# A chunked recurrence whose chain, output statistics and transposes are spread over the next pair's solver levels, with VectorE and ScalarE doing GpSimd's eight operations

## The reference

```python
def step(state, inp):                       # one token, 16 heads of 64
    r_t, w_t, k_t, v_t, kk_t, a_t = inp
    sa = jnp.einsum('bhij,bhj->bhi', state, -kk_t)
    state = (state * w_t[:, :, None, :]
             + sa[..., None] * (kk_t * a_t)[:, :, None, :]
             + v_t[..., :, None] * k_t[..., None, :])
    return state, jnp.einsum('bhij,bhj->bhi', state, r_t)
_, y = lax.scan(step, state0, (r, decay, k, v, kk, a))
y = ((y - mean) * lax.rsqrt(var + RW_GN_EPS)) * gn_w + gn_b   # per head
y = (y + sum(r * k * r_k) * v) * g
```

## Time and profile before

| what | us |
|---|---|
| median of 3 runs | 2706.45 (2702.31 to 2707.59) |
| the profiled execution's own time | 2708.74 |
| its span, first to last instruction | 2706.9 |
| TensorE busy | 2434.5 (90% of the span) |
| VectorE busy | 1606.1 (59%) |
| ScalarE busy | 634.9 (23%) |
| GpSimd busy | 563.5 (21%) |
| granted TensorE clock, mean of the span | 0.948 of full speed |

### The profile page before, as it was taken

How to read it: one execution, slowest core, us unless ns; L and a number is a source line. 1 busy time by engine, 2 the same in 40 slices (tenths; PEclk the granted TensorE clock), 3 DMA queues, 4 the chain that set the end, 5 groups by cost and what they waited for, 6 DMA issues and landing times. The chain is left out here.

```text
span 2706.9 us, 44357 instructions
## 1 busy us (share of the span) xinstructions
PE 2434.5 (90%) x16952; PEld 1977.2 (73%) x16952; DVE 1606.1 (59%) x2182; ACT 634.9 (23%) x1246; POOL 563.5 (21%) x382
## 2 busy tenths in 40 slices
PE   7999977987888869999999699999849898999998
PEld 6888865765666657888877588888638687788887
DVE  6646569945666545656556465656536565565654
ACT  3100012223545322101012310101435453210001
POOL 3212135421212102302030021213111300221213
PEclk9999997998999979999999799999969899999999
DMA  4333222430000012333325333332351101333331
GB/s 133 103 94 101 82 74 71 128 110 29 16 30 16 17 33 78 96 99 101 94 78 163 106 101 94 93 99 73 113 130 37 37 2 32 94 103 91 103 87 66
DMA packets 375943, 216.95 MB, mean 80 GB/s; under 512 B 18880, under 2 KB 359808, under 8 KB 375776
## 3 DMA queue, kind: packets, MB, share of 16 engines
q1 hardware_dynamic: 367648, 198.83, 26.0%
q10 hardware_dynamic: 8128, 15.83, 1.6%
HBM read 198.73 MB, written 15.89 MB: 79 GB/s over the span
## 5 line engine op out<-in xcount | busy, mean ns | idle before, releaser
L143 DVE TENSOR_TENSOR w_lo_ffn<-w_raw,w_hi_ffn 128x1024 fp32r<-128x1024 f32 x272 | 508.7, 1870 | 9.4
L387 POOL TENSOR_TENSOR act_ffn<-gated_ffn,usc_ffn 128x512 f32<-128x512 f32 x88 | 128.1, 1456 | 1007.4 <-ACT gated_ffn L367 1007.4
L367 ACT ACTIVATE gated_ffn<-gsc_ffn 128x512 f32<-128x512 f32 x88 | 55.8, 634 | 1010.4 <-DVE gsc_ffn L292 1010.4
L150 PE MATMUL p_gate_ffn<-hhi_ffn,w_hi_ffn 128*128 128x512 f32 x704 | 278.2, 395 | 7.6 <-DVE hlo_ffn L205 7.6
L150 PE MATMUL p_up_ffn<-hhi_ffn,w_hi_ffn 128*128 128x512 f32 x704 | 274.6, 390 | 2.9 <-DVE w_lo_ffn L143 2.9
L151 PE MATMUL p_gate_ffn<-hlo_ffn,w_hi_ffn 128*128 128x512 f32 x704 | 277.2, 394 | 0.0
L150 PE MATMUL p_down_ffn<-ahi_ffn,w_hi_ffn 128*128 128x512 f32 x704 | 274.9, 390 | 2.4 <-DVE x_res L303 2.4
L152 PE MATMUL p_gate_ffn<-hhi_ffn,w_lo_ffn 128*128 128x512 f32 x704 | 276.9, 393 | 0.0
L292 DVE TENSOR_TENSOR gsc_ffn<-p_gate_ffn,rstd_ffn 128x512 f32<-128x512 f32 x88 | 60.9, 692 | 363.6 <-PE p_up_ffn L152 363.0
L151 PE MATMUL p_up_ffn<-hlo_ffn,w_hi_ffn 128*128 128x512 f32 x704 | 274.6, 390 | 0.0
L152 PE MATMUL p_up_ffn<-hhi_ffn,w_lo_ffn 128*128 128x512 f32 x704 | 274.5, 390 | 0.0
(11 more groups left out here) (341 smaller groups left out, 4490.5 us busy)
## 6 DMA issues: line engine op xcount, KB each, us to landing
w_raw<-in_ffn_w_gate_dram SPq DMA_DIRECT2D x88, 512.0 KB, 3.8
w_raw<-in_ffn_w_up_dram SPq DMA_DIRECT2D x88, 512.0 KB, 3.8
w_raw<-in_ffn_w_down_dram SPq DMA_DIRECT2D x64, 512.0 KB, 4.1
w_raw<-in_ffn_w_down_dram SPq DMA_DIRECT2D x32, 384.0 KB, 3.4
w_raw<-in_rw_w_rkv_dram SPq DMA_DIRECT2D x24, 512.0 KB, 4.5
rkv_scratch<-staged_mix ACTq DMA_DIRECT2D x24, 256.0 KB, 2.5
w_raw<-in_kv_w_dram SPq DMA_DIRECT2D x12, 512.0 KB, 4.7
w_raw<-in_rw_w_o_dram SPq DMA_DIRECT2D x8, 512.0 KB, 5.4
```

The source lines that it names most:

```text
L143: nc.vector.tensor_tensor(lo, raw, fp(hi), ALU.subtract).then_inc(s["w_ready"], 1)
L150: nc.tensor.matmul(out, whi, hi, start=first, stop=False)
L367: nc.scalar.activation(gated[:], gsc[:, j], ACT.Silu).then_inc(s["silu"], 1)
L387: nc.gpsimd.tensor_tensor(act32[:], gated[:], usc[:, j], ALU.mult).then_inc(s["act32"], 1)
```

## The change

The recurrence is written anew as one schedule for each engine.
- The six links of pair p-1's chain, the state's part of its output and its centering now stand between the level operations of pair p. The variance of pair p-2's output comes after pair p's scores; its logarithm, exponential, normalization and gate come later in the same step; the rounded parts of pair p-3 come in level 0.
- The transposes of pair p (`turn`) are in its own levels 0 to 2, no longer in the chain of the pair before. One of them is written as 16 matmuls with an identity, so that its output lies crossed.
- Head 1's operands are put on the crossed partition halves (`side`), so that a group of 16 matmuls touches all four quadrants. One operation then serves both heads: one product, one copy, and one addition each for x and xt in a level, in separate banks.
- The first factor is an identity written ahead by ScalarE (`preset`) and four `copy_predicated` of VectorE, one of them from eight (64-column) matmuls more. Masks are applied for one level at a time (`part`). The identity in `ft` is added by 16 matmuls, and ScalarE copies `ft`.
- The mean is taken off by one matmul with a centering matrix; ScalarE squares and copies from its bank. VectorE adds the state's part to the part from inside the chunks.
- GpSimd has no block here. Of its six products VectorE takes three (`keys`, `rate_keys`), ScalarE three (as activations with scale and bias); VectorE takes the low part of the output too. ScalarE also takes the affine step after tanh from VectorE (`sg`).
- r, k, v and the weight slices have semaphores of their own and are loaded one by one. VectorE, ScalarE and TensorE wait for all constants at the start of the stage.
- The `Fori` loops in `mix_project`, `project_add` and `attention` become Python loops, so their bodies are written out.

The core of the diff:

```diff
+        def side(h, b):
+            return half(b if h == 0 else 1 - b)
...
+            def product(p, level):                       # TensorE
+                at(pe, p, "part", level + 1)
+                if level == 0:
+                    at(pe, p, "xin", 4)
+                else:
+                    at(pe, p, "x", level)
+                for t in range(NT):
+                    for b, h in quarters:
+                        m = mm(bank[side(h, b), A0 + h, cols(t)], parts[half(b), level, h, t], x[h][half(b), t], start=True, stop=True)
+                m.then_inc(s["g_mm"], 1)
...
+            def step(p):                                 # TensorE
+                scores(p); variance(p - 2); product(p, 0); chain(p - 1, 1); turn(p, 0); update(p, 0)
+                lak_v(p); chain(p - 1, 2); product(p, 1); rates(p + 1); chain(p - 1, 3); update(p, 1)
+                turn(p, 1); chain(p - 1, 4); product(p, 2); key_norm(p + 1); gate(p + 1); chain(p - 1, 5); update(p, 2)
+                turn(p, 2); chain(p - 1, 6); product(p, 3); carried(p - 1, (1, 2, 3, 4)); carried(p - 1, (5, 6, 7)); update(p, 3)
+                values(p + 1); product(p, 4); bonus(p + 1); centered(p - 1); update(p, 4); solve(p); outer(p)
...
+            def step(p):                                 # ScalarE
+                key_square(p + 1); product(p, 0); turned(p, 0); lak_v(p); rounded(p - 3); product(p, 1)
+                rates(p + 1); turned(p, 1); product(p, 2); gate(p + 1); logs(p + 1); logs_of_output(p - 2)
+                turned(p, 2); product(p, 3); roots(p + 1); decays(p + 1); roots_of_output(p - 2); values(p + 1)
+                product(p, 4); squares(p - 1); solved(p); preset(p + 1); outer(p)
...
+            def step(p):                                 # VectorE
+                scores(p); part(p, 0); key_scores(p); part(p, 1); rounded(p - 3); update(p, 0)
+                state(p - 1, 1); part(p, 2); state(p - 1, 2); update(p, 1); state(p - 1, 3); part(p, 3); state(p - 1, 4)
+                sums(p + 1); keys(p + 1); update(p, 2); state(p - 1, 5); key_norm(p + 1); state(p - 1, 6); centers(p + 1)
+                update(p, 3); part(p, 4); carried(p - 1); bonus_terms(p + 1); normalized(p - 2); gated(p - 2)
+                rate_keys(p + 1); rows_of_query(p + 1); update(p, 4); bonus(p + 1); rows_of_key(p + 1); outer(p)
...
-            with pe.Fori(0, 2) as i:                     # attention, and likewise on the other engines
+            for i in range(2):
```

More of the change, by code:

```diff
@@ new lines, in outer, with chain @@
+                m.then_inc(s["z_mm"], 1)
+            def chain(p, c):
+                if not 0 <= p < ND:
+                    return
+                if c == 1:
+                    at(pe, p, "f", 1)
+                    at(pe, p, "z", 1)
+                else:
+                    at(pe, p, "state", c - 1)
+                for h in range(2):
+                    m = mm(bank[half(h), KB, cols(c)], ft[half(h), c], zq[half(h), 0] if c == 1 else st[half(h), c], start=True, stop=True)
+                m.then_inc(s["chain"], 1)
@@ new lines, in centered @@
+            def centered(p):
+                if 0 <= p < ND:
+                    at(pe, p, "yadd", 1)
+                    mm(bank[:, EB], center[:], ysb, start=True, stop=True).then_inc(s["cen"], 1)
+            def step(p):
+                ahead = p + 1 < ND
+                scores(p)
+                variance(p - 2)
+                product(p, 0)
+                chain(p - 1, 1)
+                turn(p, 0)
+                update(p, 0)
+                lak_v(p)
+                chain(p - 1, 2)
+                product(p, 1)
+                if ahead:
+                    rates(p + 1)
+                chain(p - 1, 3)
+                update(p, 1)
+                turn(p, 1)
+                chain(p - 1, 4)
+                product(p, 2)
+                if ahead:
+                    key_norm(p + 1)
+                    gate(p + 1)
+                chain(p - 1, 5)
+                update(p, 2)
+                turn(p, 2)
+                chain(p - 1, 6)
+                product(p, 3)
+                carried(p - 1, (1, 2, 3, 4))
+                carried(p - 1, (5, 6, 7))
+                update(p, 3)
+                if ahead:
+                    values(p + 1)
+                product(p, 4)
+                if ahead:
+                    bonus(p + 1)
+                centered(p - 1)
+                update(p, 4)
+                solve(p)
+                outer(p)
@@ L941, in _ @@
+            pe.wait_ge(s["consts"], 80)
+            rates(0)
+            key_norm(0)
+            gate(0)
+            values(0)
+            bonus(0)
+            for p in range(ND):
+                step(p)
+            last = ND - 1
+            variance(last - 1)
+            for c in range(1, NC_ - 1):
+                chain(last, c)
+            carried(last, range(1, NC_))
+            centered(last)
+            variance(last)
         @block.scalar
@@ new lines, in _ @@
+            act.wait_ge(s["consts"], 80)
+            act.wait_ge(s["pv"], 2)
+            preset(0)
+            key_square(0)
+            rates(0)
+            gate(0)
+            logs(0)
+            roots(0)
+            decays(0)
+            values(0)
+            for p in range(ND):
+                step(p)
+            last = ND - 1
+            rounded(last - 2)
+            logs_of_output(last - 1)
+            roots_of_output(last - 1)
+            squares(last)
+            rounded(last - 1)
@@ new lines, in _ @@
+            key_norm(0)
+            sums(0)
+            centers(0)
+            keys(0)
+            bonus_terms(0)
+            rate_keys(0)
+            rows_of_query(0)
+            rows_of_key(0)
+            bonus(0)
+            for p in range(ND):
+                step(p)
+            last = ND - 1
+            rounded(last - 2)
+            normalized(last - 1)
+            gated(last - 1)
+            for c in range(1, NC_ - 1):
+                state(last, c)
+            carried(last)
@@ L1186, in recurrence @@
+            rounded(last - 1)
+            normalized(last)
+            gated(last)
+            rounded(last)
     close_stage(core, s)
```

871 lines of the change are left out of this document (449 added, 422 removed), and 3 rows, old and new, of the table PAIR_EVENTS.

## The result

| | us, median (lowest to highest, runs) |
|---|---|
| kernel before, same chip | 2705.3 (2701.3 to 2707.6, 7) |
| kernel after | 2689.8 (2685.3 to 2695.3, 7) |
| ratio | 0.9946, 95% interval 0.9934 to 0.9957 |
| profiled execution of after | 2688.7, span 2686.9, clock 0.946 (before 2708.7, 2706.9, 0.948) |

The change made the kernel 15.5 us faster by the medians, and 20.0 us by the two profiled executions. I had forecast 40. The time lies inside the range and the sign is right, but more than half of the expected gain is missing, and the study is about where it went.

The account below looks back on a forecast made before the run. Bound: latency passed from TensorE to ScalarE to TensorE to VectorE, no engine full. Pairs -51.6, clock +12, last pair +5.6, start -2, attention -4.5 make -40.5 us: 2668 profiled, 2666 median, range 2638 to 2695.

Parts of the forecast that it names:

- seven pairs, with the clock: First pair's scores to last pair's: 265.4 us for 317.0, -51.6, before a clock charge of 1.5 us a pair.
- last pair, with the clock: Last scores to stage end: 56.5 us for 50.9, +5.6, as the chain isn't free there; clock charged apart.
- start of the stage: Recurrence start: three transposes and their copies leave, ScalarE waits for all constants; net -2 us, between -6 and +3.
- attention, measured as all that follows the recurrence: Attention's second turn: idle TensorE (3.3 us) and VectorE (4.7 us) go on at once when unrolled; -4.5 us (0 to -5).
- The wait of `rounded`: Level 0, pairs 3 to 7: VectorE waits for ScalarE's rounding, which stands behind `lak_v`; 2.6 us a pair.
- A group of 16 matmuls (64 columns) in four quadrants costs 0.5.: TensorE's level groups: 0.5 us each, the last result some 0.25 us later.
- my walk: Step-by-step timing of a new pair from its scores to the next: 37.3 us, 39.9 with the level 0 wait.
- crossed halves don't share the array: Rival, chance 0.03: level groups keep costing 0.93 instead of 0.5, some 6 us a pair on the path; 2708 us.
- The clock (1.5 us a pair): Idle TensorE stretches before solve and in level 0: 1.5 us a pair, 12 in eight; bounds 0 and 4 a pair.
- The order before `solve`: Level 4 and after: VectorE's last addition ends 6.8 us after the product, within 12.5 us to the next scores.
- The likeliest case (0.55): The walked-through sum for the whole kernel holds: 2666 us, own range 2650 to 2682; chance 0.55.
- the queues bind more than I see: Rival, chance 0.20: in-order neighbours late at each level's handoffs, 0.75 us a level more, 26 us in all; 2692 us.

Follow-up runs that it names:

- e1: Kernel after, with ScalarE's rounding of pair p-3 moved from behind `lak_v` to the front of its step; 2664.5 us.
- e10: e9 with the first group (x) of each level update issued twice, 32 groups in all; 2667.6 us.
- e11: e9 with the second group (x^T) of each level update issued twice, 40 groups in all; 2684.0 us.
- e9: Kernel after with three edits: early ScalarE rounding, VectorE's last update ahead of the query rows, pair 6's output work behind the last pair's states; 2647.2 us.
- e7: Kernel after, with VectorE's output work of pair 6 put behind the last pair's six state operations and its addition; 2683.0 us.
- e2: Kernel after, with two unused 512-column products of constants on TensorE between the last level's matmuls and `solve`; 2682.0 us.
- e3: Kernel after, with VectorE's last level update put ahead of the query rows and the bonus product; 2675.7 us.
- e12: e9 with centering of pair p-1 moved behind the last level's matmuls and variance of pair p-2 behind the first level product; 2653.8 us.
- e4: Kernel after, with chain links and states of pairs 0 to 6 put back to the end of their own pair's step; 2706.9 us.
- e5: Kernel before with only attention's four loops written out; 2698.2 us.
- e6: Kernel after with seven operations a pair given back to GpSimd (six products or scalings and the low part); 2673.2 us.

## Why the forecast was half right, step by step

By the profiled executions the forecast was -40.5 and the measured difference -20.0. The terms:

| term | forecast | measured |
|---|---|---|
| seven pairs, with the clock | -51.6 + 10.5 = -41.1 | 298.3 - 317.0 = -18.7 |
| last pair, with the clock | +5.6 + 1.5 = +7.1 | 63.4 - 50.9 = +12.5 |
| start of the stage (0.5 of it won before the stage) | -2 | 621.9 - 626.4 = -4.5 |
| attention, measured as all that follows the recurrence | -4.5 | 1703.3 - 1712.6 = -9.3 |

The two large terms missed by 22.4 and 5.4 us. The two small ones gave 7.3 us more than forecast, most of it by a pause that I had not seen, and hid a part of the miss; that was luck.

**The wait of `rounded` (forecast 2.6 us in pairs 3 to 7).** Place, cause and pairs were right; e1 shows them. Over five pairs it measured (23.1 - 3.8 - 0.7) / 5 = 3.7 us on VectorE (two of the seven waits lie behind the last pair's step), at most 4.4, and the pairs gave back 4.9 when it went. I had started it at VectorE's idle 6.3 us, but TensorE's update lasts 1.5 us, with its dear second group, before `lak_v` can go. Over four pairs this is 19.7 for 10.4 us, though e1's first three pairs are 1.8 longer than after's, so 17.8 in all: about 7 us of the miss.

**"A group of 16 matmuls (64 columns) in four quadrants costs 0.5."** This price failed, and it is the largest miss. It is about right for x (0.52 by the timeline, 0.63 by e10). I took it for all groups, although the diff has `blocks[side(h, b)]` and `xt[side(h, b)]` both on the side to which the x^T group's result goes. So the sentence on the change that has every group of 16 touch four quadrants is wrong for this group. It uses two: 1.04 by the timeline, 0.92 by e11. Five a pair are 35 groups in seven pairs, an estimate of 35 x 0.42 = 15 us. e1's seven periods sum to 280.5, my walk without the wait and with the clock to 265.4 - 10.4 + 10.5 = 265.5. The 15 us between them are the same size; that they are these groups alone is not shown, since the clock and the order are in that sum too. The rival "crossed halves don't share the array" named this cost with another cause: crossed groups do share the array (0.52), and this group isn't crossed. The price stood in the trace of before, whose products of one head (8 matmuls) lie on the two diagonal quadrants: 0.52 us from start to start for half a group.

```profile
794.05 0.68 PE L842 MATMUL bank_rec<-xx_rec,parts_rec 64*64 64x64 f32 x16 [0.25 <-DVE xx_rec L1166]
794.57 1.33 PE L853 MATMUL bank_rec<-xx_rec,g_rec 64*64 64x64 f32 x32
```

**The clock (1.5 us a pair).** Too low for pair 4 of the kernel after. Two spells at 1.2 GHz cover 796 to 799.5 and 820 to 826.6. In the second `solve` takes 1.76 us for 1.10, and from the first outer product to the next scores it is 5.19 us, for 3.32 in e9's pair 4 at 2.4 GHz: 2.5 us for this spell alone. Both spells follow pauses that my walk had. Over the runs, pause and slow spell go together but not one to one. Where TensorE stood 2.7 to 3.0 us before `solve` (pairs 2 to 6 of after, e1 and e7), a spell began within 3 us of `solve`'s start in 15 of 15 pairs; where it stood 0.8 to 1.2 us (the same pairs of e2, e3, e9 and e12), in 6 of 20.

**The order before `solve`.** I had VectorE end its last update 6.8 us after the product and let it stand as part of the 12.5 us. It was so (TensorE stood 2.67 us), but it is a choice of order worth 12 us, not a bound.

**Last pair.** The mechanism was as written, VectorE's output work of pair 6 ahead of the first state. Forecast 58.0 with the clock, measured 63.4: the wait of `rounded(4)` was larger here as well (3.67 for 2.6 us), and the clock is 0.79. How the remaining 4 us divide is open.

**Right steps.** The predicated copies (256 columns) start 0.35 us apart in a row of three, as assumed; two table loads a pair remain, and where its input is ready the activation follows the load by 0.01 us again, so the trace still does not show the drain of about 1.38 us of which the Trainium skill speaks ("ScalarE: Activation LUTs", What ACT_TABLE_LOAD costs). Spreading the chain pays (e4, 2.7 us a pair). VectorE is busy for 27.7 us in a pair, about the 28 that I gave it, and isn't the bound. The pause at attention's turn is gone, as the -4.5 had it; the second one had not been seen, and by medians the two together gave only 4.3 us (e5).

**The rivals.** The likeliest case (0.55) named the right wait but had its own range end at 2682. The result lies in the case "the queues bind more than I see" (2692), though not by half a dozen small handoffs: as far as the runs show, by one group's price, one wait's size and the clock.

## What to carry to other kernels

When an engine with its own queue is dropped, its operations bring their waits along: put each one where its input is already there, not where its result would be in time. Here the low part's input was one line late in another engine's order, and that line was worth more than the change. Price a quadrant group by where both its operands and its result lie, not by its count, and ask of every matmul in a queue whether it stands where the engine waits anyway (free) or where it doesn't (full price), before moving it "out of the way". Count an idle stretch on TensorE with what may follow it: here the clock fell behind each pause of 2.7 to 3.0 us before `solve`, and in pair 4 that cost 2.5 us beside the pause.

## What the hardware showed that I had not expected

- VectorE's own instructions are slower while GpSimd works: the scan took 2107 ns on average with GpSimd's seven operations in the kernel and 1213 without, the part products 895 and 682 ns. Within e6 only the part products that overlap a GpSimd instruction were slow (0.77 to 1.66 us; the others 0.68 or 0.69).
- Sixteen matmuls of 64 x 64 by 64 columns cost 0.52 us in four quadrants and 1.04 in the two diagonal ones, at 2.4 GHz (0.63 and 0.92 us each when a kernel makes them twice).
- The pauses next to `solve` don't settle what clock is granted behind it. In pair 4, e9 and e12 have nearly the same ones (1.17 and 0.97 us before `solve`, then 1.20 us before the outer products), and e9 stayed at 2.4 GHz while e12 was granted 0.50 from 808.5 to 811.5 us. What decides stays open.
- Engines stood idle for 3.3 to 4.7 us in the second turn of a loop, at two places, for nothing the profile shows; with the loop written out both were gone.
